# A decoder layer on one core: feed-forward started at once, down products spread between gate and up products, cached pages reordered by GpSimd

## The reference, cut to what matters

```
x <- LN1(alpha*x + 0.5*SwiGLU_a(x))     # the first feed-forward
x <- LN2(alpha*x + Mix(x))              # projection, short conv, three attention branches
x <- LN3(alpha*x + 0.5*SwiGLU_b(x))     # the second feed-forward
SwiGLU(x) = (silu(x @ w_gate) * (x @ w_up)) @ w_down        # 1024 -> 2816 -> 1024
# part of Mix, from the caches alone:
past_cmp = cmp_pool[page_table]          # 8 sequences x 32 pages, 128 KB each
hid = silu(einsum('nbcgp..d,cpdh->nbcgh', blocks + pe, cmp_w1)); kc, vc = hid @ cmp_w2
```

## Time and profile before

| | us |
|---|---|
| median of 3 runs | 1609.25 (1608.97 to 1612.55) |
| the profiled execution, its own time | 1610.04 |
| its span, first to last instruction | 1608.3 |
| PE busy | 1447.8 (90%) |
| DVE busy | 521.5 (32%) |
| ACT busy | 410.7 (26%) |
| POOL busy | 117.4 (7%) |

### The profile page before, as it was taken

How to read it: one execution, slowest core, us unless ns; L and a number is a source line. 1 busy time by engine, 2 the same in 40 slices (tenths; PEclk the granted TensorE clock), 3 DMA queues, 4 the chain that set the end, 5 groups by cost and what they waited for, 6 DMA issues and landing times.

```text
span 1608.3 us, 32780 instructions
## 1 busy us (share of the span) xinstructions
PE 1447.8 (90%) x13241; PEld 1353.6 (84%) x13241; DVE 521.5 (32%) x746; ACT 410.7 (26%) x635; POOL 117.4 (7%) x151
## 2 busy tenths in 40 slices
PE   1599999999999998899888879876989999999996
PEld 0599899999999998899856556555879999999995
DVE  0000033333233334522334434435453333233334
ACT  0000022221122212422214434431252222122214
POOL 0000000000000000308050202200030000000000
PEclk9999999999999999999979999997999999999998
DMA  8837513233223331233393526522122233233311
GB/s 216 276 124 240 175 29 91 83 96 93 81 78 91 99 101 35 61 84 92 75 313 117 173 80 218 173 62 79 53 66 84 86 108 87 66 91 91 103 54 56
DMA packets 250514, 176.14 MB, mean 110 GB/s; under 512 B 21635, under 2 KB 246642, under 8 KB 249812
## 3 DMA queue, kind: packets, MB, share of 16 engines
q1 hardware_dynamic: 228948, 150.10, 32.4%
q10 hardware_dynamic: 18432, 16.79, 3.2%
q0 software_dynamic: 3072, 8.39, 1.6%
HBM read 171.29 MB, written 8.10 MB: 112 GB/s over the span
## 4 chain that ended last, share of the span: by engine, by line
PE 85%; ACT 4%; DVE 3%; DMA 3%; issue 2%; ACTq 1%; SPq 0%; DVEq 0%
PE ps L603 61%; PE ps L633 9%; PE ps L901 2%; PE ps L886 2%; PE ps L932 2%; PE ps L691 2%; DMA pe_sb<-in_cmp_pe_dram 2%; DMA w1p<-in_cmp_w_dram 1%; ACT kt L1214 1%; ACTq L335 1%; PE ps L969 1%; ACT x L1096 1%; PE ps L948 1%; PE ps L702 1%; PE ps L911 1%
## 5 line engine op out<-in xcount | busy, mean ns | idle before, releaser
L603 PE MATMUL ps<-xh,ghi 128*128 128x272 f32 x1904 | 399.6, 291 | 22.0 <-DVE xl L1422 13.4
L603 PE MATMUL ps<-xh,glo 128*128 128x272 f32 x1904 | 397.2, 290 | 0.0
L603 PE MATMUL ps<-xl,ghi 128*128 128x272 f32 x1904 | 395.7, 290 | 0.0
L603 PEld LDWEIGHTS ps<-xh,ghi 128*128 128x128 f32 x1904 | 302.6, 190 | 26.5 <-issue 21.0
L603 PEld LDWEIGHTS ps<-xl,ghi 128*128 128x128 f32 x1904 | 302.6, 191 | 0.0
L603 PEld LDWEIGHTS ps<-xh,glo 128*128 128x128 f32 x1904 | 300.4, 191 | 0.0
L1278 DVE TENSOR_TENSOR glo<-graw,ghi 128x1024 fp32r<-128x1024 f32 x119 | 147.5, 1242 | 267.8 <-ACT ghi L1035 266.8
L633 PE MATMUL ps<-span 64*64 64x128 f32 (+1 forms) x2560 | 148.9, 415 | 0.0
L633 PEld LDWEIGHTS ps<-span 64*64 64x64 f32 x2560 | 142.0, 156 | 5.5
L603 PE MATMUL ps<-hh,dhi 128*128 128x272 f32 x704 | 145.4, 287 | 0.0
L603 PE MATMUL ps<-hl,dhi 128*128 128x272 f32 x704 | 145.3, 287 | 0.0
(11 more groups left out here) (296 smaller groups left out, 1210.8 us busy)
## 6 DMA issues: line engine op xcount, KB each, us to landing
page<-in_cache_sel_kv_dram SPq DMA_DIRECT2D x192, 128.0 KB, 3.0
span<-in_cache_cmp_kv_dram ACTq DMA_DIRECT2D x128, 128.0 KB, 3.9
span<-in_cache_cmp_kv_dram SPq DMA_DIRECT2D x128, 128.0 KB, 3.9
graw<-in_ffa_gate_dram SPq DMA_DIRECT2D x22, 512.0 KB, 3.8
graw<-in_ffa_up_dram SPq DMA_DIRECT2D x22, 512.0 KB, 3.8
draw<-in_ffa_down_dram SPq DMA_DIRECT2D x16, 704.0 KB, 4.6
graw<-in_w_in_dram SPq DMA_DIRECT2D x44, 256.0 KB, 3.2
graw<-in_ffb_gate_dram SPq DMA_DIRECT2D x22, 512.0 KB, 3.8
```

Of the source, the lines that this page charges most:

```text
L603: last = nc.tensor.matmul(out[:, h, 0:HALF], a[:, k, :], b[:, k, h * HALF:(h + 1) * HALF], start=(k == 0 and a is hi and b is xhi), stop=( ...
```

## The change

- **Opening.** x is loaded first, then the first gate and up tile. The parameters, page numbers and small weights follow. x is transposed between the chunks of the first gate product, and ACT and DVE split it straight out of PSUM.
- **Feed-forward, both.** No halves. `hh`, `hl` hold two tiles. The down weights come row by row, four DMAs of 128 KB for a tile into two buffers, and are split in 128 x 128 blocks with two buffers of each part. While tile i's gate and up products run, the 8 down products of tile i - 1, one chunk each (m = 0 to 7), stand between their chunks: m = 0 after the gate's 4th chunk, m = 1 after the 6th, m = 2 after the 8th, m = 3 to 6 after the up product's 2nd, 4th, 6th and 8th, and m = 7 after the 2nd chunk of the next gate product. Each is added to x by itself, so `add_y` runs 176 times in a feed-forward, where it ran 16 times.
- **SP's order.** For tile i: gate load, up load, the four down loads of tile i - 1 and, in 16 of the 22 tiles of the first feed-forward, four quads of pages. A quad is one read of 4 page numbers and 4 DMAs of 128 KB into one of two landing buffers. All 256 page loads are now on SP's queue.
- **Cached pages.** GpSimd copies each quad from its landing buffer into `perm`, where the pages of one feature lie side by side, and frees the buffer (`permuted`). There are four groups of 64 pages. `hidden_cached` for a group (256 matmuls, 130 columns, the last of each 65 being the bias) stands ahead of tiles 5, 11 and 17, the fourth inside the first norm.
- PSUM banks are moved to suit, and the projection's first pair is taken out of its loops.

```diff
+GP = 2 * NPG
+GROUPS = NB * NPG // GP
+QUAD = 4
+PW = GP + 1
+AFTER = (4, 10, 16)
+LOADS = (1, 6, 12, 18)
...
+            _, numbers = nc.values_load_multi_w_load_instructions(
+                pages_sb[0:1, DS(first, QUAD)], engines=[eng.engine], min_val=0, max_val=NPHYS - 1,
+                skip_runtime_bounds_check_because="the DMA itself checks its bounds")
+            for k, page in enumerate(numbers):
+                eng.dma_start(landing[b][:, k:k + 1, :], cache_cmp[0, DS(page, 1)].rearrange("o p c g d -> p o (c g d)")
+                              ).then_inc(dma_landing[b], 16)
...
             def ffn_loads(n, gate, up, down_w):
...
+                uses = USES[("ffa", "ffb")[n]]
+                def gate_up(s, i):
+                    w = (gate, up)[s]
+                    col = value(i * 128)
+                    free_from(w_lo[s], i + (uses[s] + ONE))
+                    sp.dma_start(graw[s][:], w[0].rearrange("(k p) f -> p k f", p=128)[:, :, DS(col, 128)]
+                                 ).then_inc(dma_w[s], 16)
+                def down(i):
+                    row = value(i * 128)
+                    for k in range(4):
+                        last = (n * FT) * 4 + k - 2 + 1
+                        free_from(d_lo[1], i * 4 + (last + ONE))
+                        sp.dma_start(draw[k % 2][:].rearrange("p a b -> p (a b)"),
+                                     down_w[0, DS(row, 128), k * 256:(k + 1) * 256]).then_inc(dma_d[k % 2], 16)
+                def body(i, j=None):
+                    gate_up(0, i)
+                    gate_up(1, i)
+                    down(i - 1)
+                    if j is not None:
+                        for k in range(GP // QUAD // 4):
+                            free_from(permuted, j * 4 + (k - 1 + ONE))
+                            landing_loads(sp, k % 2, value(j * (4 * QUAD) + k * QUAD))
+                gate_up(0, 0)
+                gate_up(1, 0)
+                if n == 0:
+                    params()
+                    done = 1
+                    for g, first in enumerate(LOADS):
+                        if first > done:
+                            with sp.Fori(done, first) as i:
+                                body(i)
+                        if g == 0:
+                            body(1, 0)
+                            compress_weights()
+                            with sp.Fori(2, 5) as i:
+                                body(i, i - 1)
...
+                else:
+                    sp.wait_ge(std_ready, 4)
+                    with sp.Fori(1, FT) as i:
+                        body(i)
...
+            for g in range(G):
+                pool.tensor_copy(perm[:, g:2 * G:G, :, GP], pe_sb[:])
+            for j in range(NB * NPG // QUAD):
+                g, at = divmod(j * QUAD, GP)
+                if g and at == 0:
+                    pool.wait_ge(q["hid_in_psum"], g)
+                pool.wait_ge(dma_landing[j % 2], (j // 2 + 1) * QUAD * 16)
+                pool.tensor_copy(perm[:, :, :, at:at + QUAD].rearrange("p x d a -> p a x d"),
+                                 landing[j % 2][:].rearrange("p a (x d) -> p a x d", d=HD)).then_inc(permuted, 1)
...
+            def hidden_cached(bank, d0, d1):
...
                     for h, c in ((0, 0), (1, 1), (0, 1), (1, 0)):
-                        rows, col = slice(h * BLK, (h + 1) * BLK), c * 128 + d
...
-                            cpages[g][rows, :, col:col + HD + 1:HD].rearrange("p a g -> p g a"),
-                            start=(d == 0), stop=(d == HD - 1))
-                last.then_inc(q["hid_in_psum"], 1)
+                            ps[c * HD:(c + 1) * HD, bank + h, 0:G * PW], w1[rows, c, d, :],
+                            perm[rows, c * G:(c + 1) * G, d, :], start=(d == 0), stop=(d == HD - 1))
...
-                        for s in range(2):
-                            use = (2 * n + half) * (KC // 2)
-                            pe.wait_ge(d_lo[s], i + (use + 1) + ONE)
-                            pe.wait_ge(y_added[s], i + use + ONE)
-                            product(ps[:, 4 + 2 * s:6 + 2 * s, :], dhi[s], dlo[s], hh, hl, FH,
-                                    last_h=before + FH + ONE).then_inc(d_used[s], 1)
+                before = n * FT
+                def down(i, par, m):
+                    s = m % 2
+                    use = 4 * before + m // 2
+                    pe.wait_ge(d_lo[s], i * 4 + (use + 1 + ONE))
+                    pe.wait_ge(y_added[s], i * 4 + (use + ONE))
+                    if m == 0:
+                        pe.wait_ge(hl_ready, i + (before + 1 + ONE))
+                    for a, b in ((dhi[s], hh[par]), (dhi[s], hl[par]), (dlo[s], hh[par])):
+                        for h in range(2):
+                            last = nc.tensor.matmul(ps[:, 4 + 2 * s + h, 0:HALF], a[:], b[:, h * HALF:(h + 1) * HALF],
+                                                    start=(a is dhi[s] and b is hh[par]), stop=(a is dlo[s]))
+                    last.then_inc(d_used[s], 1)
...
+                def tile(i, par, ready=None, older=True, old=True, group=None, first=None):
+                    def step(c):
+                        if c == 2 and older:
+                            if group is not None:
+                                pe.wait_ge(q["hid_ready"], group + 1)
+                            down(i - 2, par, KC - 1)
+                        if c >= 4 and c % 2 == 0 and old:
+                            m = c // 2 - 2
+                            if group is not None and m == 2:
+                                pe.wait_ge(y_added[1], 4 * (before + i - 1) + 1 + ONE)
+                                compressed(group)
+                            if group is not None and m == 3:
+                                pe.wait_ge(q["kc_ready"], group + 1)
+                            down(i - 1, 1 - par, m)
+                    pe.wait_ge(w_lo[0], i + (uses[0] + 1 + ONE))
+                    pe.wait_ge(sg_ready, i + (before + ONE))
+                    product(ps[:, 0:2, :], ghi[0], glo[0], xh, xl, KC, ready, step if first is None else first
+                            ).then_inc(w_used[0], 1)
+                    step(KC)
+                    pe.wait_ge(w_lo[1], i + (uses[1] + 1 + ONE))
+                    pe.wait_ge(ht_ready, i + (before + ONE))
+                    product(ps[:, 2:4, :], ghi[1], glo[1], xh, xl, KC, None, lambda c: step(KC + c)
+                            ).then_inc(w_used[1], 1)
+                    step(2 * KC)
+                if n == 0:
+                    for k in range(3):
+                        transposed(k)
...
+                            pe.wait_ge(permuted, (g + 1) * GP // QUAD + ONE)
+                            pe.wait_ge(q["dma_cmp_w"], 16 * 4)
+                            pe.wait_ge(q["dma_first"], 16 * 5)
+                            pe.wait_ge(y_added[1], 4 * (i - 2) + 3 + ONE)
+                            hidden_cached(6, 0, HD)
+                        tile(i, i % 2, group=g)
+                else:
+                    pe.wait_ge(std_ready, 4)
+                    tile(0, 0, (norm_lo, KC), False, False)
+                    tile(1, 1, None, False)
...
+                if last_hidden:
+                    pe.wait_ge(permuted, GROUPS * GP // QUAD + ONE)
+                    pe.wait_ge(sg_ready, FT + ONE)
+                    hidden_cached(0, 0, 24)
                 pe.wait_ge(csum_step, (KC + 1) * (n + 1))
...
+                    if last_hidden:
+                        hidden_cached(0, (24, 48)[h], (48, HD)[h])
...
+            def split_d(i, m):
+                k, s = m // 2, m % 2
+                act.wait_ge(dma_d[k % 2], i * 32 + (16 * (k // 2) + 16))
+                act.wait_ge(d_used[s], i * 4 + (k + ONE))
+                act.activation(dhi[s][:], draw[k % 2][:, s, :], ACT.Copy).then_inc(d_hi[s], 1)
...
+                def tile(i, par, old=True, more=True, group=None):
+                    if old:
+                        copy_h(i - 1, 1 - par)
+                        split_w(1, i + uses[1], (i + (fills[1] + 1)) * 16)
+                        split_d(i + (before - 1), 0)
+                        if group is not None:
+                            hid_values(group, 6)
+                        for m in (1, 2, 3):
+                            split_d(i + (before - 1), m)
+                    act.wait_ge(w_used[0], i + (uses[0] + 1))
+                    act.activation(sg[par][:].rearrange("p (h t) -> p h t", h=2), ps[:, 0:2, 0:HALF],
+                                   ACT.Silu).then_inc(sg_ready, 1)
+                    if more:
+                        split_w(0, i + (uses[0] + 1), (i + (fills[0] + 2)) * 16)
+                    if old:
+                        for m in range(4, KC):
+                            split_d(i + (before - 1), m)
...
+                def tile(i, par, older=True, old=True, more=True, group=None):
+                    if old:
+                        gated(i - 1, 1 - par)
```

(100 more changed lines are left out.)

488 lines of the change are left out of this document (190 added, 298 removed).

## The result

The changed kernel takes 1854.6 us (median of 5 runs, 1849.68 to 1865.34) where the kernel before took 1609.66 on the same chip: 1.152 times as long, 95% interval 1.149 to 1.155.

What follows compares the result with a forecast made beforehand. PE was taken to bound both feed-forwards, with late gate loads now stopping it: first feed-forward +236, norm +21, second feed-forward +90, together +347 on 1610.04, giving 1956 us after a 0.8 correction to the median; range 1800 to 2170.

Steps and rivals of the forecast that it cites:

- Opening: Start of the kernel: x lands at about 9.5, gate product ends at 24.5, tile 1 begins at 34 us.
- Steady tile: Feed-forward tile without pages: PE waits 2.3 us at m = 4 for a late gate load; 22.0 us, bounds 20.35 and 23.6.
- Tile with pages: First feed-forward, 16 tiles: four quads issued ahead of the gate load make it 15.3 us later; 38.1 us a tile.
- Clock: PE's granted clock after each pause: half speed for 3 to 6.5 us, taken as 2.3 us lost a restart.
- my sign that it is 0.50 after each pause: Sign of being right: in the first feed-forward, PE's granted clock is 0.50 after each pause.
- Compression: Page products in four groups of 256 matmuls: 27 us a group, between 18.6 and 37.4.
- my sign of 36 to 73 ns a page matmul: Sign of being right: page matmuls of the compression take 36 to 73 ns each.
- First feed-forward: Whole stage, from the opening through 22 tiles and hidden groups: ends at 865 instead of 628.4 us, +236.
- (c): Rival, page tiles: GpSimd copies at 9.2 ns a number, 12 us more in 15 tiles; 2136 us, chance 0.17.
- (b): Rival, feed-forwards: pages cost nothing, the gate load is late only by the down buffers; 1692 us, chance 0.06.
- (a): Rival, feed-forwards: gate loads are in time, the order having been misread; 1523 us, chance 0.07.
- The rule on issue time: Page loads: spreading DMAs over engines saves only issue time; pages would cost their bytes, 8 us a tile, sum 1845.

Runs made afterwards that it cites:

- experiment 1: Changed kernel with SP issuing the gate load of tile i + 1 ahead of the up and down loads of tile i: 1645.98 us.
- experiment 4: Kernel before, with the page matmuls' moving operand read from neighbouring numbers (unit step, other numbers multiplied): 1568.18 us.
- experiment 2: Changed kernel with all page loads issued by GpSimd, only weights left in SP's list: 1717.34 us.
- experiment 5: Changed kernel with SP's load list written in the order of need, nothing else changed: 1504.6 us, 0.935 of the kernel before.
- experiment 7: experiment 5 with page copies by ScalarE, first two hidden groups one tile later, last page group one earlier, quads in pairs: 1489.45 us, 0.925 of the kernel before.
- experiment 9: experiment 7 with the compression's weights loaded by GpSimd in sixteen 256 KB pieces instead of by SP in four of 1 MB: 1495.06 us.
- experiment 6: Changed kernel with the gate load one tile ahead and all page loads issued by GpSimd: 1527.59 us.

## Why the prediction was right, and where its sizes were off

The direction and the mechanism were right, at the place that the prediction named: block m = 4 waits for its split, behind the gate's, behind a load that SP issues after the fourth down load and the pages. The time, 1854.6, is 101 below the forecast of 1956, inside the range. Two terms fell below their own lower bounds, the copy and the groups; the second feed-forward cost more than was forecast.

- **Opening.** Tile 1 was to begin at 34; tile 0 ended at 35. Block m = 4 of tile 1 was forecast at 82.7 and came at 83.9.
- **Steady tile.** Forecast 22.0. In the second feed-forward PE comes to m = 4 at 1356.39 in tile 1 and at 1792.04 in tile 20: 22.9 a tile. That is 4.9 over 18.04, in 20 tiles 98 us; the stage lost 107.7 where 90 was forecast. The other 10 lie at its beginning and in its last blocks at DVE's pace, not divided further. That the loss is the order and not the two down buffers alone is shown by experiment 1, which keeps both buffers and has 414 us.
- **Tile with pages.** Forecast 38.1, measured 34.1. From the fourth down load to the gate load SP took 12.2 us (308.01 to 320.22) where I had 15.3: the copy was 2.0 and not 3.3, the landing 2.1 and not the 3.0 of the earlier trace rows, and a quad's issue about 2.5 and not 2.9. The row for the copy was the wrong neighbour: it came from arithmetic with 512 numbers, and the new copy lies below even my lower bound of 2.3. My estimate of 2.5 from the Trainium skill, GPSIMD Engine Reference, section Performance pitfalls for Q7 kernels, was nearer, and still high; its 2.9 cycles are for reads with a wide step, and here the reads are packed.
- **Clock.** I had 2.3 us a restart. In the tile with pages the 96 matmuls from 292.80 to 306.57 took 13.8 us, 1.7 more than at 0.1253 each. The granted clock was 0.50 after that pause. In the second feed-forward it was 0.50 after the pause that ended at 1401.5 and 1.00 after the one that ended at 1424.3, so my sign that it is 0.50 after each pause did not hold. In the earlier trace rows I also read the rise at 1108.3; a mean of 0.67 in that microsecond puts it at 1108.7, which changes the term's lower end by 0.2.

```profile
294.00:296.00 2.00, 2.00 (x11) 2.00 (x10) 0.93 (x2) 0.31 (x1) 0.00 (x0) 0.50 0.22 66
1403.00:1405.00 2.00, 2.00 (x11) 2.00 (x10) 0.78 (x2) 0.16 (x1) 0.00 (x0) 0.50 0.20 66
1424.30:1426.00 1.70, 1.69 (x13) 1.69 (x14) 1.42 (x3) 0.31 (x1) 0.00 (x0) 1.00 0.00 0
```

- **Compression.** Forecast 27 us a group, bounds 18.6 and 37.4; measured 14.5 (58.1 / 4, 28 ns for each of 2048 records), below the lower bound. That bound came from 64 columns with the 1 KB step, which experiment 4 shows to be no floor for 128 columns with unit step. So my sign of 36 to 73 ns a page matmul was missed too.
- **First feed-forward.** +134.7 against +236, 101 less. From m = 4 to m = 4 the fourteen page tiles after the first are 4.0 shorter on the mean, 55 in all. Tiles 5, 11 and 17 with their groups took 37.5, 36.8 and 38.3 where I had 51 each: 40. From m = 4 of tile 20 to the end it is 43.3 where I had 51.1: 8. Tile 1 and tiles 10 and 16 give 3 back. PE idles 14.3 us in the page tile shown (34.10 less 19.76), a little under my 15 to 20. The norm is +9.5 and not +21 because the fourth group is shorter as well.
- **Rivals.** (c), the slow copy, fell by the copy's row. The mechanisms of (b) and (a) became experiments 2 and 5: 1717 where (b) said 1692, 1505 where (a) said 1523 with groups of 29 us. (a) had the direction right: once the loads are in time the change is a gain. That its number is so near is luck. With groups 12.5 shorter and the norm at +9.5 its sum is 1474, 31 below experiment 5 and 15 below experiment 7. In experiment 7 PE comes to m = 4 of tiles 1 to 4 at distances of 21.8, 23.3 and 21.3 us and in the later tiles with pages at 18.0 to 18.3, so some 12 of its 15 lie in the first tiles, where the 1 MB loads of `cmp_w1` go out too. What holds PE up there is left open; experiment 9, which moved these loads, did not gain.
- **The rule on issue time** (the Trainium skill, DMA: Bandwidth & Descriptors, section Issuing engines are not separate DMA queues). By it the sum was 1845, 10 us from the result, but the runs do not bear out its reason: SP needed 12.2 us a tile for the quads where I had estimated 8 for their bytes, and experiment 2, which moved only the issue and the waits in front of it, gave 137 us back. The agreement is chance, made of a shorter copy and shorter groups.

What the order cost in the changed kernel is then told by runs: 209 of the 245 us come back with the gate load alone moved, and 350 with the whole list in order of need. So the change as a whole, with its loads in that order, is worth about 105 us, and the order that it came with took 350. How the 105 divide among the opening, the compression and the rest is not shown.

## What to carry to other kernels

When a schedule of compute is woven more finely, write the load list anew: for each load, note when its buffer comes free and when its data are due, and put nothing that waits late ahead of something that is due early in the same queue. A gain and a loss can come in one change; a forecast of "slower" with a named wait is also a plan for the faster kernel. Before a copy is given to an idle engine, look at what its neighbours read at that moment.

## What the hardware showed that I had not expected

- A matmul record of 64 x 64 weights with 128 to 130 float32 columns takes 28 to 34 ns with unit step of the moving operand and 72 with a step of 1 KB.
- A copy of 1,024 float32 numbers that writes 64 at a step of 260 bytes takes 2.0 us on GpSimd and 2.11 on ScalarE; ScalarE's packed copy of as many takes 1.05 (the gate splits).
- GpSimd's copy stretched VectorE's split from 0.28 to 2.04 us. In experiment 5 it went the other way as well: a gate split that began 0.19 us before the copy kept its 1.22, and the copy took 3.04.

```profile
219.77 1.22 DVE L1386 TENSOR_TENSOR glo<-graw,ghi 128x1024 fp32r<-128x1024 f32 x1
219.96 3.04 POOL L598 COPY perm<-landing 128x1024 f32<-128x1024 f32 x1 [2.88 <-DMA landing<-in_cache_cmp_kv_dram]
```

In these rows the one that began first kept its length. In experiment 6, however, the gate split had begun at 208.64 and the copy at 209.03, and it was the split that came out at 3.40. GpSimd's spans are rough in such records, so who began first there is not certain.
